# Reordering what stands between the page loop and the first expert gather in a two-layer hybrid step (SSM, latent attention, retrieved experts)

## The reference

```
h    = rmsnorm(x);  proj = h @ w_in               # gates, z, xbc, dt, c_q, c_kv, k_rope
A    = ssd branch (conv, chunked scan, gated norm) @ w_ssm_proj
B    = latent attention: o_lat = softmax(scores) @ latents, for each of 8 heads
       o = o_lat @ w_vb (per head);  B = o @ w_mla_proj
x    = x + (sigmoid(gate_a) * A + sigmoid(gate_b) * B) @ w_out
h    = rmsnorm(x)
q    = h @ peer_wq            # 8 heads x 256; two halves, each against 128 keys
       top 16 of each half -> 16 x 16 candidates -> top 16: 16 experts a head
x    = x + sum over heads, k of  softmax(score) * gelu(u[idx] . h) * v[idx]
```

## Time and profile before

| | |
|---|---|
| median of 3 runs | 2412.59 us (2412.56 to 2417.77) |
| profiled execution | 2414.14 us, span of its instructions 2412.6 us |
| PE busy (matmul) | 2003.7 us, 83% of the span |
| DVE busy | 1514.5 us, 63% |
| ACT busy | 449.2 us, 19% |
| POOL busy | 649.1 us, 27% |
| moved by DMA | 744.52 MB, 309 GB/s over the span |

### The profile page before, as it was taken

How to read it: one execution, slowest core, us unless ns; L and a number is a source line. 1 busy time by engine, 2 the same in 40 slices (tenths; PEclk the granted TensorE clock), 3 DMA queues, 4 the chain that set the end, 5 groups by cost and what they waited for, 6 DMA issues and landing times. The chain is left out here.

```text
span 2412.6 us, 26529 instructions
## 1 busy us (share of the span) xinstructions
PE 2003.7 (83%) x9014; PEld 1150.0 (48%) x9014; DVE 1514.5 (63%) x3803; ACT 449.2 (19%) x1356; POOL 649.1 (27%) x592
## 2 busy tenths in 40 slices
PE   6999887988988877777779998889788888778775
PEld 4887655744444422222258876557344443222221
DVE  2454433278777788888525444333786877887874
ACT  1234211021211111111022332101211111111111
POOL 0000000044443444444200000000444434444441
PEclk9999899989999999999979998989899999999998
DMA  4446389189999999999744374871999999999996
GB/s 162 124 143 231 122 286 306 64 347 416 412 416 393 400 386 420 420 420 413 293 155 150 116 248 140 277 269 58 399 414 413 415 377 418 393 420 420 420 416 251
DMA packets 206115, 744.52 MB, mean 309 GB/s; under 512 B 16338, under 2 KB 96650, under 8 KB 137856
## 3 DMA queue, kind: packets, MB, share of 16 engines
q0 software_dynamic: 83008, 581.14, 58.9%
q1 hardware_dynamic: 122960, 161.59, 20.6%
HBM read 731.40 MB, written 11.46 MB: 308 GB/s over the span
## 5 line engine op out<-in xcount | busy, mean ns | idle before, releaser
L996 PE MATMUL ps<-arena 128*128 128x512 f32 (+1 forms) x2112 | 1012.3, 612 | 243.5 <-DVE arena L1551 243.2
L2019 POOL DMA_INDIRECT arena<-in_peer_uv,arena x528 | 614.9, 1165 | 909.9 <-PE ps L996 726.6
L1542 DVE CUSTOM_DVE_ANT_0 arena<-arena,h 128x1024 f32<-128x1024 f32 x512 | 627.8, 1226 | 252.1 <-DMA arena<-in_peer_uv,arena 244.6
L996 PEld LDWEIGHTS ps<-arena 128*128 128x128 f32 (+1 forms) x2112 | 366.9, 187 | 855.3 <-DVE arena L1551 540.9
L471 PE MATMUL ps<-ht_tok,wring 128*128 128x264 f32 (+2 forms) x1792 | 396.0, 378 | 19.9 <-DMA wring<-in_peer_wq 14.0
L471 PEld LDWEIGHTS ps<-ht_tok,wring 128*128 128x128 f32 x1792 | 325.5, 195 | 89.4 <-issue 17.4
L1832 ACT ACTIVATE arena<-arena 128x1 f32<-128x1 f32 x528 | 105.2, 203 | 1018.9 <-DVE arena L1542 1017.8
L1551 DVE TENSOR_SCALAR arena<-consts,arena 128x128 f32<-128x128 f32 (+1 forms) x528 | 181.4, 344 | 21.1 <-ACT arena L1832 21.1
L2005 POOL DMA_DIRECT2D nrow<-in_norm_ffn x2 | 1.1, 536 | 347.4 <-PE ps L787 347.4
L471 PE MATMUL ps<-arena,wring 128*128 128x264 f32 x384 | 91.2, 393 | 2.2 <-DMA wring<-in_w_mla_proj 1.1
L471 PEld LDWEIGHTS ps<-arena,wring 128*128 128x128 f32 x384 | 71.9, 191 | 16.6 <-DVE arena L1022 2.0
(11 more groups left out here) (312 smaller groups left out, 1791.3 us busy)
## 6 DMA issues: line engine op xcount, KB each, us to landing
arena<-in_pages SPq DMA_DIRECT2D x256, 272.0 KB, 4.1
wring<-in_w_in SPq DMA_DIRECT2D x38, 1024.0 KB
wring<-in_peer_wq SPq DMA_DIRECT2D x20, 1024.0 KB
arena<-in_peer_uv,arena POOLq DMA_INDIRECT x528, 12.1
h<-in_state_ssm POOLq DMA_DIRECT2D x16, 512.0 KB, 5.1
out<-h POOLq DMA_DIRECT2D x16, 512.0 KB, 5.0
wring<-in_w_ssm_proj SPq DMA_DIRECT2D x8, 1024.0 KB
arena<-in_w_out SPq DMA_DIRECT2D x8, 1024.0 KB, 12.6
```

Of the source, the lines that this page charges most:

```text
L996: last = pe.matmul(ps[0:outs, SUM_BANK[t] + half, :], diag[:, n % DIAGS, 0:outs], ring[:, n % RING, D_MODEL + half * 512:D_MODEL + (half + ...
L1542: dve.tensor_tensor_reduce(ring[:, k, 0:D_MODEL], ring[:, k, 0:D_MODEL], tokens, 1.0, 0.0, ALU.mult, ALU.add, dots[:, column(n)]).then_inc ...
L2019: pool.indirect_dma_start(ring[:, k, :], None, table, bass.IndirectOffsetOnAxis(ap=idx[:, TOPK * u + j:TOPK * u + j + 1], axis=0)).then_in ...
```

## The change

Nothing is computed differently but for the shape of the samples' mix. What moves:

- `heads_out` of tile 0 goes into half sample 15 of the page loop; the last pieces of `prompt_values` go behind `half_turns` of halves 13 to 15 (`PROMPT_LATER`).
- Behind the loop come `mla(0..7)` for tile 0's columns alone, the turn of the half sums between 3 and 4, then `out(0..3, 0)`, with the turn of the weights behind the first.
- The samples' mix becomes 16 matmuls with 32 columns of weights against 256 latent columns, a copy (`smix`) and 4 turns; it stands behind `out(3, 0)`. `heads_out` and `mla` for tile 1 and the samples (136 columns) stand among the norm, `queries(0)`, `scores(0)` and the steps of `best_experts(0)`; so do `out(0, 1)` and `out(1, 1)`. `out(2, 1)`, `out(3, 1)`, the samples' sums, the norm of tiles 1 and 2, `queries(1)`, `scores(1)` and the turned rows go behind the indices, most of them into slots 0 to 6 (`late_tiles`, `later_rows`).
- Unit 0's slots run no step of unit 1 up to slot 4, then four a slot.
- SP issues `mla_block(1)` ahead of the four `w_out` loads, each with its own semaphore; query block 0 gets a place of its own (`wq0`) and is issued behind them.
- The gathers' places are permuted (`HOME`); gather 0 waits for the indices alone, gather 2 for tile 1's heads, gathers 3 and 5 for `out_samples(0)` and `(1)`.

```diff
+HOME = (0, 1, 7, 2, 3, 4, 5, 6)
+ROW_CHUNKS = ((0, 3), (3, 3), (6, 2))
...
+    for first in range(3):
+        steps[4 + first] = [("rows", first)]
     for hh in range(2, P_HEADS):
         begun = TOPK * (hh - 2) - (2 if hh == P_HEADS - 1 else 0)
...
+        at = (2, 6, 10) if hh > 2 else (7, 10, 13)
...
-    15: [("values", (1, 0, 0))], 16: [("values", (1, 0, 1)), ("values", (1, 1, 0)), ("values", (1, 1, 1))],
+    15: [("heads", (0,)), ("heads", (1,)), ("heads", (2,)), ("heads", (3,))],
 }
+PROMPT_LATER = {13: [(1, 0, 0)], 14: [(1, 0, 1)], 15: [(1, 1, 0), (1, 1, 1)]}
...
+                    def heads_out(q, lo, hi):
+
+                        if q == 0:
+                            pe.wait_ge(sem("aux_free"), 4 + marks["mixed", min(lo, 1)])
+                        b = aux.fill()
+                        for k in range(2):
+                            hh = 2 * q + k
+                            for c in range(2):
+                                last = pe.matmul(ps[k * 64:k * 64 + 64, b, 0:hi - lo], wvb[:, c, hh * 64:(hh + 1) * 64], ol[:, c, hh, lo:hi],
+                                                 start=c == 0, stop=c == 1)
+                        aux.filled(last)
+                        marks["heads", min(lo, 1)] = aux.n
+
+                    def mla(m, lo, hi):
+
+                        if m == 0:
+                            pe.wait_ge(sem("aux_free"), 4 + marks["heads", min(lo, 1)])
+                        if m % 4 == 0:
+                            if lo == 0:
+                                state["mla", m] = next_block(4, 2 * BLOCK)
+                            state["fresh"] = (m == 0) == (lo == 0)
+                        w = state["mla", m - m % 4]
+                        b = aux.fill()
+                        aux.filled(product(ps[:, b, 0:hi - lo], lambda c: w[:, c, (m % 4) * P:(m % 4 + 1) * P], lambda c: ot[:, c, lo:hi], 4))
...
+                    for m in range(4):
+                        mla(m, 0, P)
+                    pe.wait_ge(sem("half_sums"), 1)
...
+                    for m in range(4, DC):
+                        mla(m, 0, P)
...
                     pe.wait_ge(sem("mixed"), 1)
-                    for k in range(4):
+                    out(0, 0)
+                    pe.wait_ge(sem("sample_weights"), 1)
...
+                    for k in range(1, 4):
                         out(k, 0)
                     marks["x", 0] = aux.n
...
+                    pe.wait_ge(sem("sample_mix"), 1)
+                    b = aux.fill()
+                    for j in range(2):
+                        for weights, rows in ((f_wd, lambda s: obs[:, s, :]), (f_wn, lambda s: lat[0:SAMPLES, 2, :])):
+                            for g in range(4):
+                                last = pe.matmul(ps[32 * g:32 * g + 32, b, j * KV_LORA:(j + 1) * KV_LORA], weights[:, 4 * j + g, :], rows(4 * j + g),
+                                                 start=weights is f_wd, stop=weights is f_wn, skip_group_check=True)
+                    aux.filled(last)
...
+                    for q in range(4):
+                        heads_out(q, P, TOKENS)
                     pe.wait_ge(sem("ph_ready"), 1)
...
+                    mla(0, P, TOKENS)
+                    mla(1, P, TOKENS)
                     pe.wait_ge(sem("aux_free"), 4 + marks["turned", 0])
                     queries(0, 0, 0, P)
                     queries(0, 1, 0, P)
...
+                    mla(2, P, TOKENS)
+                    scores(0, (0,))
+                    for m in range(3, DC):
+                        mla(m, P, TOKENS)
+                    pe.wait_ge(sem("mixed"), 2)
+                    out(0, 1)
+                    out(1, 1)
+                    out_samples(0)
...
+                    out(2, 1)
+                    out(3, 1)
+                    out_samples(1)
...
+                    def mla_gated(m, lo, hi):
+
+                        b = aux.read()
+                        aux.emptied(dve.tensor_tensor(gate[:, DC + m, lo:hi], gate[:, DC + m, lo:hi], ps[:, b, 0:hi - lo], ALU.mult), wait=m % 4 == 3)
+                        if m % 4 == 3:
+                            last = dve.tensor_tensor(gate[:, m - 3:m + 1, lo:hi], gate[:, m - 3:m + 1, lo:hi], gate[:, DC + m - 3:DC + m + 1, lo:hi], ALU.add)
+                            if m == DC - 1:
+                                last.then_inc(sem("mixed"), 1)
...
                     first = best_experts(0)
...
+                    for m in range(3, DC):
+                        for _ in range(2):
+                            next(first)
+                        mla_gated(m, P, TOKENS)
+                    for k in range(2):
+                        for _ in range(4):
+                            next(first)
+                        out(k, 1)
                     for _ in first:
                         pass
...
+                    def late_tiles(n):
+
+                        if n == 0:
+                            out(3, 1)
+                            copy4(hp[2][:, 512:1024])
+                        elif n == 1:
+                            for half in range(2):
+                                b = aux.read()
+                                xs = x[0:SAMPLES, 2, half * 512:(half + 1) * 512]
+                                aux.emptied(dve.tensor_tensor(xs, xs, ps[0:SAMPLES, b, :], ALU.add))
+                        elif n == 2:
+                            px_mean(1, slice(46, 48))
+                        elif n == 3:
+                            px_rows((1, 2))
+                        elif n == 4:
+                            then(dve.memset(qz.rearrange("p s c -> p (s c)"), 0.0))
...
-                        for _ in range(3 if u != SAMPLE_UNIT else 6):
+                        late_tiles(n)
+                        for _ in range(6 if u == SAMPLE_UNIT else 3 if u else 4 if j > 4 else 0):
...
+                        if n == 1:
+                            queries_out(1, 0, 0, P)
+                            queries_out(1, 1, 0, P)
+                            act.wait_ge(sem("aux_free"), 4 + marks["x", 1])
+                            squares(hp[1], x[:, 1, :], st[:, 46:47])
+                            squares(hp[2], x[:, 2, :], st[:, 47:48], "px1_squares")
+                        elif n == 2:
+                            scores_out(1, (0,))
+                            root(st[:, 49:51], st[:, 46:48], "px1")
...
                     mla_block(0)
+                    mla_block(1)
...
-                    mla_block(1)
...
+                    sp.dma_start(wq0, w_q[:, :, 0:BLOCK]).then_inc(sem("wq0_load"), 16)
...
-                        if n == 0:
-                            pool.wait_ge(sem("aux_full"), marks["x", 1])
+                        if n == 2:
+                            pool.wait_ge(sem("aux_full"), marks["heads", 1])
+                        elif n in (3, 5):
+                            pool.wait_ge(sem("aux_full"), marks["sums", n // 5])
```

More of the change, by code:

```diff
@@ L268 @@
 ])
+share(ARENA_PEER, "wq0", ARENA_PEER["sc"][0] + 1024, DC * BLOCK)
+assert ARENA_PEER["wq0"][0] >= ARENA_ATT["ql"][0] and ARENA_PEER["wq0"][1] <= ARENA_ATT["ql"][1]
 share(ARENA_ATT, "wout01", S1 + SLOT_COLS, 2 * DC * BLOCK)
@@ L837, in _ @@
                                 prompt_turns(*at)
+                            elif piece == "heads":
+                                heads_out(*at, 0, P)
                             else:
@@ L879, in _ @@
-                    aux.all_emptied()
-                    for k in range(2):
-                        w = next_block(4, 2 * BLOCK)
-                        for m in range(4):
-                            b = aux.fill()
-                            aux.filled(product(ps[:, b, 0:TOKENS], lambda c: w[:, c, m * P:(m + 1) * P], lambda c: ot[:, c, :], 4))
-                    marks["wq_block"] = state["n"]
                     def out(k, t):
                         t0, rows = TILES[t]
+                        if t == 0:
+                            pe.wait_ge(sem(f"wout{k}_load"), 16)
@@ L940, in _ @@
+                    aux.filled(last)
+                    pe.wait_ge(sem("aux_free"), 4 + aux.n)
+                    b = aux.fill()
+                    for k in range(4):
+                        last = turn(ps[:, b, k * P:(k + 1) * P], smix[:, k * P:(k + 1) * P], P)
+                    aux.filled(last)
+                    marks["mixed", 1] = aux.n
+                    for q in range(4):
+                        heads_out(q, P, TOKENS)
                     pe.wait_ge(sem("ph_ready"), 1)
@@ L1290, in _ @@
                     then(dve.memset(mla("pts"), 0.0))
+                    then(dve.memset(dtb[0:SAMPLES, 0:SAMPLES * 32], 0.0))
                     def ssm(m):
@@ L1385, in _ @@
                     then(dve.tensor_reduce(f_dif[:, 4, :], f_new.rearrange("p b h -> p h b"), AX.X, ALU.add))
+                    for m in range(4):
+                        mla_gated(m, 0, P)
                     b = aux.read()
@@ L1448, in _ @@
```

(7 more changed lines are left out.)

190 lines of the change are left out of this document (86 added, 104 removed).

## The result

The changed kernel takes 2397.78 us, the median of 7 runs (2391.31 to 2404.26); the kernel before took 2413.87 (2406.44 to 2417.77, 7 runs) in the same comparison. The ratio is 0.994 with a 95% interval of 0.9924 to 0.9956: faster by 11 to 18 us. The profiled run took 2396.4 us with a span of 2394.9, so 17.7 less than the span before. The forecast was 2396.1 for the profiled run and 2395 for the median.

What follows compares the result with a forecast made beforehand. Gathers and peer_wq blocks on full DMA engines set the end, a PE and DVE chain their start. Gather 0 13.5 us earlier, less 3.5 and 0.8, gives 9 us a layer, 18 off 2414.14: 2396.1, median 2395 (range 2379 to 2412).

Steps and rivals of the forecast that it cites:

- The first `mla` at 415.0: Page loop's end: from the last pages at 404.73, PE's remaining work brings the first mla to about 415.0, not 432.82.
- Block 1 lands at 422.4, PE idles 3.6 us, and the clock falls: Ahead of mla 4: w_mla_proj's block takes 6.5 us (bounds 4.6 and 7.5); half clock then loses 2 us.
- `out(3, 0)` done at 443.3, rows normed 448.9, scores 458.4: First tile's chain: out(3, 0) 19.4 us earlier than 462.74, then 5.6 us to normed rows and 9.5 to scores.
- Gather 0 at 478.7: First gather: 20.3 us behind the scores instead of 11.4, yet 13.5 us earlier than before (bounds 9 and 18).
- The first slots: Work moved behind gather 0: samples' sums about 485.5, gather 8 near 495, px_rows near 503, outputs(3) at 505 to 507.
- the half clock beyond `out(0, 1)`: Sign of a wrong forecast: PE's half clock, expected at first in out(0, 1), lasting past it.
- The stream gives back 4.3 us a layer: Gathers' stream: 3.5 us of gaps and 0.8 for later heads come off the 13.5 us lead, leaving 9 a layer.
- gathers 19 to 23 leave gaps of 3.5 us in all: Slots' stream: these gathers, issued behind slot 10's queries and slot 13's scores, come late; gathers 0 to 18 never do.
- 24 and 2 blocks: Traffic counted until gather 23 has landed, at 2.5 us each: 549.3 with 3.5 us of gaps, before 559.2.
- (2): Rival: the stream takes no gap and no clock falls; 14 to 17 us a layer gained, 2381 us; chance 0.23.
- (3): Rival: block 1 3 us later, half speed through both out, wout3 late; lead 4 us, no change, 2411; chance 0.20.
- (4): Rival: PE on half clock through second tile's rows and queries of slots 3 to 15; 13 us slower, 2426; chance 0.12.

Runs made afterwards that it cites:

- e2: Changed kernel with gather 0 also waiting for the samples' last sums, out_samples(1): 2422.45 us, ratio 1.0033 to the kernel before.
- e6: Changed kernel with SP issuing block 1 of w_mla_proj behind the four w_out loads again, the old order: 2404.12 us, ratio 0.9951 to the kernel before.
- e8: Changed kernel where, from slot 40 of each layer, a gather waits for the slot five before it, not eight: 2551.68 us, ratio 1.0561.
- e9: Changed kernel with query block 2 issued once the second tile's last mla product has ended, not once query block 1 is begun: 2400.38 us, ratio 0.9941.
- e1: Changed kernel with block 1 of w_mla_proj issued once the last SSM product has ended, not once block 0 is begun: 2383.4 us, ratio 0.9879.
- e5: Changed kernel with 9 unused PE products ahead of each of its two new waits, before mla(4) and before mixed 2: 2395.26 us, ratio 0.9928.
- e7: Changed kernel with e1, e3 and e5's unused products ahead of the wait for mixed alone: 2383.76 us, ratio 0.9862 to the kernel before.
- e10: Changed kernel with the edits of e7 and e9 together: 2372.39 us, ratio 0.9829 to the kernel before.
- e3: Changed kernel with ACT's squares and root of the second norm ahead of its query and score copies in slots 1 and 2: 2397.77 us, ratio 0.9934.

## Why the prediction was right, step by step

**The first `mla` at 415.0.** It started at 411.26. The last pages were 2 us earlier in this run (half sample 15's scores at 402.77, not 404.73), and from there it took 8.5 us, not the 10.3 of the sum: the head outputs took 2.02 us, not 2.8 (a term taken between 2.5 and 5.6 from a row that was partly at the low clock, and the clock was whole), and the other terms were 1 us too large. The forecast was 3.7 us too late. In the seven other runs whose PE lists are alike up to there (e2 to e6, e8, e9) those 8.5 us return, and the pages end anywhere from 402.55 to 408.77.

**Block 1 lands at 422.4, PE idles 3.6 us, and the clock falls.** The block was there at 421.46, near the forecast by luck: it was issued at 411.92 and took 9.5 us to land, where the sum has 6.5 and its bounds end at 7.5. In those 9.5 us 3.2 MB moved, the block and the keys (2.1 MB) that the sum counted and also the norm's row (0.5 MB) and a part of the first `w_out` loads (0.6 MB). So PE waited 6.14 us (6.89 in layer 2), not 3.6. The burst behind it took 5.70 us, which is the predicted 3.8 and 2 for the clock; over all runs with the wait it is 5.3 to 6.7. e1 shows that this one wait is worth 9.4 / 7.1 us of lead and 14 us of the time. It was in the sum as a term of 5.6 us a layer, too small by 2.5, and it was the largest thing that the change left undone. The rule of the Trainium skill that was weighed here (TensorE: Matmul & The Clock Gate, HAM oscillation) was borne out by both new waits, though only the first is for a DMA: the clock was 0.50 at 422 and again from 467 to 473. In e5 products ahead of a wait helped where they lasted to its end, and not where they ended 3.2 us before it.

**`out(3, 0)` done at 443.3, rows normed 448.9, scores 458.4.** Measured 442.6, 448.63 and 458.71. Each sum of this stretch held within a microsecond.

**Gather 0 at 478.7.** It came at 479.94. It is 1.2 us late, and the half clock, which lasted longer than its term, accounts for that: the two `out` took 10.23 us and not 8.8, and DVE stood 5.52 us on the first of them where the forecast named 3. In layer 2 they took 8.86, the forecast's value. The 8.7 us from the scores to "mixed" don't follow from the terms given there, which add up to 7.6; 8.3 were measured. Predicted earlier by 13.5, measured 12.25 and 15.5, or 10.3 and 15.7 by the last scores of the page loop. That the moment was met to 1.2 us in layer 1 is in part luck: the early first `mla` (3.7 us) and the slow block (3 us) nearly cancelled.

**The first slots.** Gather 5 was due with the samples' sums at 485.5 and came at 488.33; gather 8 at 495, and came at 496.49; `px_rows` was to end near 503, and ended at 503.11; `outputs(3)` between 505 and 507, and started at 504.56. With the drain that the Trainium skill gives (ScalarE: Activation LUTs, What ACT_TABLE_LOAD costs) these would have been later; here, too, the root started at the load's end (498.90 and 1.28, then 500.19), and none shows. PE's work in the slots ended at 542.3 (forecast 542 to 544), and from there PE waits for DVE. From 482 to 505 the stream ran at 400 GB/s with a share of 0.99: the ring's cushion took these delays. One sign of being wrong did show, the half clock beyond `out(0, 1)`: PE waited 4.04 us ahead of `outputs(3)`, and the first two slots behind it took 6.75 us where the sum has 1.99 each.

**The stream gives back 4.3 us a layer.** It gave back 5.3 and 3.9. The size is right and the place is right, the step's mechanism is not: "gathers 19 to 23 leave gaps of 3.5 us in all". The rows show no gaps. The stream slows to 364 to 370 GB/s with the engines shown busy (25 us at 369 instead of 413 GB/s are 1.1 MB, an estimated 2.7 us). Late gathers with few in flight are the cause that fits: e8 shows that fewer places alone lower the rate at a share of 0.95, and the slow stretch is gone in e7 and e10, where the gathers come earlier. And "24 and 2 blocks" was counted alike for both sides, though the change itself moves a block of 0.9 MB from ahead of the stream into it: the sum left out SP's third query block, whose issue waits until the second is begun, now behind gather 0 (e9). Its 0.92 MB are an estimated 2.2 us of the 5.3. e9 shows that taking it out gains nothing by itself, since the late gathers cover it, and e10 that it counts as soon as they are gone. So the sum came out right with one cause half named, late gathers but as gaps, and one left out; that the two make up 4.3 us a layer is luck.

**The rivals.** (2), no gaps and no clock falls, is refuted by the clock of 0.50 and by the stream's 5.3 us; e10, which removes both, gives 2372, better than that rival's 2381, as it also removes the wait for block 1. (3), a chain that keeps the lead, wanted block 1 later by 3 us, the half clock through both `out`, and `wout3` late. Counted from its issue the block was 3 us slower than taken, and 3.2 us instead of 1.8 were lost in the two `out` of layer 1; the early first `mla` hid the one, the other was half of what the rival takes, and no wait for `wout3` shows. So this rival was nearer than its 0.20 makes it look. (4), the half clock through slots 3 to 15, is refuted: `outputs(3)` and the turned rows behind it ran at 0.50 until about 511, and from 512 on it was 1.00.

**What stays open.** Which part of e7 it is that shortens the stream once the block is gone, the second norm ahead of the copies or the whole clock in `out(0, 1)`, was not taken apart; e3's layer 1 speaks for the norm (3.5 us). Nor is it shown why few gathers in flight lower the rate, or from which number on: e10 has 2.2 on average in the same 20 us and runs at full rate, the changed kernel has 1.9 and doesn't.

## What to carry to other kernels

When a full stream follows a chain, the first transfer's start is worth its whole lead, and it is cheap to test by itself: hold it back and see whether the end moves with it. Read the rate of a "full" stretch beside its share, and count the bytes on every queue between two marks on both sides of a change, since a queue's next wait can push a transfer across the mark. If two edits for one stretch each show nothing, run them together before they are dropped: here the norm moved ahead (e3) and the early block (e9) gained nothing alone. With e1's edit, which is worth 14 us by itself, e7 has 14 and e10, with both, 25 (each by its median against that of the changed kernel).

## What the runs showed of the hardware

- A DMA share of 0.95 to 1.00 went with 362 to 370 GB/s where few gathers of 1 MB were in flight (1.4 to 1.9 on average), and with 406 to 426 elsewhere (e8: 362 against 409 over 550 us).
- 9 products without use, which ended 3.22 us before the wait did, left the next burst at 0.50 and 6.74 us; 9 that lasted through a wait of 4 us kept it whole (7.17 us instead of 8.86 to 10.23).
- The end of the page loop varies between runs of kernels that are alike up to there: the first `mla` of layer 1 started between 411.05 and 417.3, which is a good part of the 10 us or so that the runs of one kernel differ by.
